# Delta rule of a two-block network: the chunk inverse as two 64-token diagonal blocks

## What is computed

```python
def _gdn_scan(q, k, v, log_a, beta, s0):
    g = jnp.cumsum(log_a.reshape(b, h, n, CHUNK), axis=-1)
    rel = g[..., :, None] - g[..., None, :]
    a = jnp.einsum('bhnid,bhnjd->bhnij', kc, kc) * bc * jnp.where(strict, jnp.exp(jnp.where(strict, rel, 0.0)), 0.0)
    rhs = jnp.concatenate([bc * vc, bc * jnp.exp(g)[..., None] * kc], axis=-1)
    sol = lax.linalg.triangular_solve(a + jnp.eye(CHUNK, dtype=a.dtype), rhs,
                                      left_side=True, lower=True, unit_diagonal=True)
    u, wk = sol[..., :dv], sol[..., dv:]
    ...
    def step(s, inp):
        v_new = u_n - jnp.einsum('bhck,bhkv->bhcv', w_n, s)
        s_next = jnp.exp(gl_n)[..., None, None] * s + jnp.einsum('bhck,bhcv->bhkv', kt_n, v_new)
        return s_next, (None if q is None else (v_new, s))
```

## Time and profile before

| | us |
|---|---|
| median of 3 runs (lowest, highest) | 3285.2 (3284.71, 3288.44) |
| profiled execution, first to last instruction | 3281.3 |
| PE busy | 2868.6 (87%) |
| DVE busy | 977.1 (30%) |
| POOL busy | 599.6 (18%) |
| ACT busy | 460.3 (14%) |
| the delta rule's stretch, 377.6 to 764.5 | 386.9 |

### The profile page before, as it was taken

The page is one execution under the profiler, slowest core; times in us unless marked ns, Lnnn a source line. Parts: engine busy times, 40 slices in busy tenths (PEclk is TensorE's granted clock), DMA queues, the critical chain, the costliest instruction groups (busy, mean ns, idle before and its releaser), DMA issues.

```text
span 3281.3 us, 34289 instructions
## 1 busy us (share of the span) xinstructions
PE 2868.6 (87%) x14021; PEld 1432.4 (44%) x14021; DVE 977.1 (30%) x1607; ACT 460.3 (14%) x959; POOL 599.6 (18%) x431
## 2 busy tenths in 40 slices
PE   5998699998998989997999789677888889889887
PEld 2644577774443555443454333344232233223232
DVE  2043555552113341111111258663111121121122
ACT  2012122221101211111111211341000000000000
POOL 0001255551200123433443210311000000000000
PEclk7999899999998899998999889888899999999999
DMA  5020243322312359997999721124899999999997
GB/s 228 26 77 0 68 132 125 123 94 109 115 51 99 138 213 384 374 383 263 388 375 364 279 83 51 36 99 164 323 421 421 421 421 421 421 421 421 421 421 292
DMA packets 127316, 793.24 MB, mean 242 GB/s; under 512 B 21795, under 2 KB 22179, under 8 KB 56761
## 3 DMA queue, kind: packets, MB, share of 16 engines
q1 hardware_dynamic: 102328, 744.31, 56.5%
q0 software_dynamic: 23008, 37.81, 4.8%
q10 hardware_dynamic: 1824, 8.91, 0.7%
HBM read 769.37 MB, written 38.86 MB: 246 GB/s over the span
## 4 chain that ended last, share of the span: by engine, by line
PE 58%; DMA 26%; DVE 8%; issue 3%; ACT 3%; POOL 1%; SPq 0%; POOLq 0%; ACTq 0%; DVEq 0%
DMA arena<-in_w_down 12%; PE b L2928 9%; DMA yd<-arena 8%; PE b L1389 5%; PE b L1825 4%; PE b L489 4%; DMA arena<-h2d,arena 3%; PE b L2963 3%; PE b L491 3%; PE b L2416 2%; PE b L630 2%; PE b L1839 2%; PE b L1077 2%; PE b L1090 2%; PE b L1453 2%
## 5 line engine op out<-in xcount | busy, mean ns | idle before, releaser
L2928 PE MATMUL b<-arena 128*64 128x512 f32 x2048 | 456.8, 603 | 17.9 <-DMA arena<-in_w_up 7.1
L1825 PE MATMUL b<-arena 128*64 128x256 f32 x3072 | 355.6, 384 | 2.9 <-DMA arena<-in_w_gu 1.6
L2943 PE MATMUL b<-arena 128*64 128x512 f32 x1024 | 244.7, 602 | 57.6 <-DMA arena<-in_w_down 57.3
L2928 PEld LDWEIGHTS b<-arena 128*64 128x64 f32 x2048 | 155.1, 138 | 315.7 <-issue 273.8
L1825 PEld LDWEIGHTS b<-arena 128*64 128x64 f32 x3072 | 213.0, 137 | 114.4 <-issue 4.6
L2142 POOL DMA_INDIRECT yd<-arena x96 | 152.5, 1588 | 344.0 <-ACT arena L1923 138.0
L1839 PE MATMUL b<-arena 128*64 128x512 f32 x768 | 186.0, 604 | 0.7 <-issue 0.7
L2098 DVE TENSOR_TENSOR arena<-arena,b 128x128 f32<-128x128 f32 x96 | 27.9, 290 | 515.1 <-ACT arena L1916 515.1
L1389 PE MATMUL b<-arena 128*128 128x512 f32 x384 | 167.0, 596 | 9.7 <-DMA arena<-in_w_in 9.7
L2943 PEld LDWEIGHTS b<-arena 128*64 128x64 f32 x1024 | 64.8, 135 | 236.8 <-DMA arena<-in_w_down 138.0
L3035 DVE TENSOR_TENSOR arena<-arena,b 128x512 f32<-128x512 f32 x32 | 20.6, 686 | 462.8 <-PE b L2928 462.8
(11 more groups left out here) (473 smaller groups left out, 3724.0 us busy)
## 6 DMA issues: line engine op xcount, KB each, us to landing
arena<-in_w_gu SPq DMA_DIRECT2D x65, 2048.0 KB, 13.1
arena<-in_w_gate SPq DMA_DIRECT2D x128, 1024.0 KB, 27.0
arena<-in_w_up SPq DMA_DIRECT2D x128, 1024.0 KB, 26.1
arena<-in_w_down SPq DMA_DIRECT2D x128, 1024.0 KB, 24.5
arena<-in_w_dn SPq DMA_DIRECT2D x65, 1024.0 KB, 10.4
arena<-in_w_mod SPq DMA_DIRECT2D x80, 512.0 KB, 3.8
arena<-in_w_in SPq DMA_DIRECT2D x19, 2048.0 KB, 8.4
arena<-yd SPq DMA_DIRECT2D x12, 512.0 KB, 8.9
```

The source lines that it names most:

```text
L1825: x = e.matmul(ps[i % 2][64 * j:64 * j + 64, 0:256], XGT[i % 2][:, k % 4, (k // 4) * 64:(k // 4) * 64 + 64], GUB[place_of(w)][:, k, j * 25 ...
L2928: x = e.matmul(ps[b + c][64 * hf:64 * hf + 64, :], XS[q % 2][:, kb, (n % 2) * 64:(n % 2) * 64 + 64], w[:, u * 512:(u + 1) * 512], start=(k ...
L2943: x = e.matmul(ps[4][64 * hf:64 * hf + 64, :], H[:, c * 4 + j, hi * 64:hi * 64 + 64], w[:, i * 1024 + hf * 512:i * 1024 + hf * 512 + 512], ...
```

## The change

The inverse is made of 64-token blocks. The two diagonal 64x64 blocks of each head's matrix go through the ladder's levels 1 to 5, each on its own half of the partitions, with X and XT side by side in one tile `XX` (4 heads x 64 columns each), so that one DVE subtraction takes both. Then level 6 makes the off-diagonal block alone, as two groups of four 64x64 products, which ACT writes with a minus sign into a full-size transposed inverse `XTF`. W is gone: keys times state (`KS`, phase 14, on PE) is scaled by -beta*exp(g) and added to the scaled values by DVE before the inverse is applied, and V is one product a head. Each tick now does the ladder's groups of all units first (`..._small`) and then the rest (`..._large`). LAG is 6, and there are 84 ticks. The level masks are 64 columns wide, and there are six levels of them, so the constants have 896 columns fewer. The decay differences are made with whole-tile DVE instructions in place of eight quarter ones, Q is moved to phase 3, and DVE clears the two `XTF` tiles once at the start.

The core of the diff:

```diff
-    for n, s in enumerate((1, 2, 4, 8, 16, 32, 64)):
-        same = (r // (2 * s)) == (c // (2 * s))
+    for n, s in enumerate((1, 2, 4, 8, 16, 32)):
+        same = (r64 // (2 * s)) == (c64 // (2 * s))
...
-    LAG, PHASES = 7, 18
+    LAG, PHASES = 6, 18
...
             for n, ph in under_way(tick):
-                pe_phase(e, n, ph)
+                for u in small_uses(n, ph):
+                    pe_small(e, n, u)
+            for n, ph in under_way(tick):
+                for u in large_uses(n, ph):
+                    pe_large(e, n, u)
             if tick < len(rows.pieces):
                 rows.pe(e, tick)
...
+        if kind == "P" and lv < 6:
+            e.wait_ge(*pool_.at(n, "BT", lv))
+            e.wait_ge(*dve.at(n, ("XX", lv - 1)))
+            for h in range(4):
+                for b in range(2):
+                    x = e.matmul(p[half(b), half(h)], BT[half(b), half(h)], X[half(b), half(h)], start=True, stop=True, skip_group_check=True)
+        elif kind == "P":
+            e.wait_ge(*dve.at(n, ("XX", 5)))
+            for h in range(4):
+                x = e.matmul(p[far, half(h)], B["off"][near, half(h)], X[near, half(h)], start=True, stop=True, skip_group_check=True)
+        elif lv < 6:
+            e.wait_ge(*act_.at(n, ("P", lv)))
+            for h in range(4):
+                for b in range(2):
+                    if lv < 5 or b == d:
+                        e.matmul(p[half(b), half(h)], XT[half(b), half(h)], P[half(b), half(h)], start=True, stop=True, skip_group_check=True)
+            for h in range(4):
+                for b in range(2):
+                    x = e.matmul(p[half(b), 256 + 64 * h:320 + 64 * h], P[half(b), half(h)], XT[half(b), half(h)], start=True, stop=True, skip_group_check=True)
...
-                x = e.matmul(p[:, hs(h)], B["bk"][:, hs(h)], B["XT"][:, hs(h)], start=True, stop=True)
...
+        elif u == "KS":
+            p = free(e, n, "KS")
+            e.wait_ge(*dve.at(n - 2, "S"))
+            for h in range(4):
+                x = e.matmul(p[:, hs(h)], KT[:, h, tsl], S_[d][:, hs(h)], start=True, stop=True)
...
             for h in range(4):
-                x = e.matmul(p[:, hs(h)], B["XT"][:, hs(h)], B["bv"][:, hs(h)], start=True, stop=(s == 0))
-                if s:
-                    x = e.matmul(p[:, hs(h)], B["wT"][:, hs(h)], S_[d][:, hs(h)], start=False, stop=True)
...
+                x = e.matmul(p[:, hs(h)], XTF[d][:, hs(h)], B["bv"][:, hs(h)], start=True, stop=True)
...
+            for b in range(2):
+                e.activation(h64(B["AA"][half(b), 256:512]), p[half(b), :, half(b)], ACT.Copy).then_inc(*act_.up(n, "blocksT", b))
+            e.activation(h64(B["off"][half(d), :]), p[half(d), :, half(1 - d)], ACT.Copy).then_inc(*act_.up(n, "T"))
...
+            e.tensor_tensor(heads(B["ET"]), heads(p[:, :]), per_row(B["g"], 4, 128), ALU.subtract).then_inc(*dve.up(n, "rel"))
+            e.wait_ge(*dve.now())
+            e.tensor_scalar(B["A"], B["ET"], 0.0, None, ALU.max).then_inc(*dve.up(n, "A"))
+            e.tensor_scalar(B["ET"], B["ET"], 0.0, None, ALU.min).then_inc(*dve.up(n, "ET"))
...
+            e.tensor_tensor(h64(B["BT"]), h64(B["AA"][:, 256:512]), by4(C[f"{mT}{lv}"]), ALU.mult).then_inc(*pool_.up(n, "BT", lv))
```

More of the change, by code:

```diff
@@ L995, in uses @@
             return ["g", "G"]
[L996 to L1010 removed]
+        if ph in (1, 2):
+            return ["KT"[ph - 1]]
+        if ph == 3:
+            return ["Q"] if t < 4 else []
+        if ph == 14:
+            return ["KS"] if s else []
+        if ph == 16:
+            return ["V"]
+        if ph == 17:
+            return (["O"] if t < 4 else []) + (["S"] if s < 5 else [])
+        return []
+    order = [(n, u) for tick in range(ticks) for uses in (small_uses, large_uses) for n, ph in under_way(tick) for u in uses(n, ph)]
     bank = {x: ps[i % 7] for i, x in enumerate(order)}
@@ L1018, in evacuated @@
             e.wait_ge(*act_.at(n, "EG"))
-        elif u in ("T", "W") or u[0] == "P" or (u == "O" and first[units[n][2]] == n):
+        elif u == "T" or u[0] == "P" or u == ("XX", 6) or (u == "O" and first[units[n][2]] == n):
             e.wait_ge(*act_.at(n, u))
@@ L1114, in pe_phase @@
         else:
             e.wait_ge(*dve.at(n, "V"))
[L1116 to L1126 removed]
+            p = free(e, n, "S")
@@ L1128, in act @@
+            for h in range(4):
+                x = e.matmul(p[:, hs(h)], B["kt"][:, hs(h)], B["vn"][:, hs(h)], start=True, stop=True)
+        x.then_inc(*mm.up(n, u))
     def act(e):
@@ L1131, in act, with act_small, act_large @@
             for n, ph in under_way(tick):
-                act_phase(e, n, ph)
-    def act_phase(e, n, ph):
+                for kind, lv in small_uses(n, ph):
+                    act_small(e, n, kind, lv)
+            for n, ph in under_way(tick):
+                act_large(e, n, ph)
+    def act_small(e, n, kind, lv):
+        s, d, t = units[n]
+        B = sets[n % 3]
+        p = bank[n, (kind, lv)]
+        if kind == "P":
+            r = slice(0, 128) if lv < 6 else half(1 - d)
+            e.wait_ge(*mm.at(n, ("P", lv)))
+            e.activation(B["A"][r, 0:256], p[r, 0:256], ACT.Copy).then_inc(*act_.up(n, ("P", lv)))
+        elif lv == 6:
+            r = half(d)
+            e.wait_ge(*mm.at(n, ("XX", 6)))
+            e.activation(heads(XTF[d])[r, :, half(1 - d)], h64(p[r, 0:256]), ACT.Copy, scale=-1.0).then_inc(*act_.up(n, ("XX", 6)))
+    def act_large(e, n, ph):
         s, d, t = units[n]
@@ L1162, in dve_, with dve_small, dve_large @@
         all_of(e, *K.ret)
+        for d in range(2):
+            e.memset(XTF[d], 0.0).then_inc(*dve.up("clear", d))
         for tick in range(ticks):
             for n, ph in under_way(tick):
-                dve_phase(e, n, ph)
+                dve_small(e, n, ph)
+            for n, ph in under_way(tick):
+                dve_large(e, n, ph)
             if tick < len(rows.pieces):
                 rows.take(e, tick)
-    def dve_phase(e, n, ph):
+    def dve_small(e, n, ph):
+        s, d, t = units[n]
+        B = sets[n % 3]
+        XX = B["XX"]
+        if ph == 3:
+            a = CCOLS["lev0" if d == 0 else "levT0"][0]
+            pair = K.CT[:, a:a + 128].rearrange("p (u o n) -> p u o n", u=2, o=1).broadcast_to([128, 2, 4, 64])
+            e.wait_ge(*act_.at(n, "blocksT", 1))
+            e.tensor_tensor(XX.rearrange("p (u h n) -> p u h n", u=2, h=4), B["AA"].rearrange("p (u h n) -> p u h n", u=2, h=4), pair,
+                            ALU.mult).then_inc(*dve.up(n, "X0"))
+            e.wait_ge(*dve.now())
+            e.tensor_tensor(XX.rearrange("p (a n) -> p a n", a=8), per_col(C["eye"], 8), XX.rearrange("p (a n) -> p a n", a=8),
+                            ALU.subtract).then_inc(*dve.up(n, ("XX", 0)))
+        elif 4 <= ph < 12 and ph % 2:
+            u = ("XX", (ph - 3) // 2)
+            e.wait_ge(*mm.at(n, u))
+            e.tensor_tensor(XX, XX, bank[n, u][:, :], ALU.subtract).then_inc(*dve.up(n, u))
+        elif ph == 13:
+            u = ("XX", 5)
+            p = bank[n, u]
+            e.wait_ge(*mm.at(n, u))
+            r = half(d)
+            e.tensor_tensor(XX[r, 0:256], XX[r, 0:256], p[r, 0:256], ALU.subtract).then_inc(*dve.up(n, "X5"))
+            if n >= 2:
+                e.wait_ge(*mm.at(n - 2, "V"))
+            else:
+                e.wait_ge(*dve.at("clear", d))
+            e.tensor_tensor(heads(XTF[d])[half(0), :, half(0)], h64(XX[half(0), 256:512]), h64(p[half(0), 256:512]), ALU.subtract).then_inc(*dve.up(n, "XT5"))
+            e.tensor_tensor(heads(XTF[d])[half(1), :, half(1)], h64(XX[half(1), 256:512]), h64(p[half(1), 256:512]), ALU.subtract).then_inc(*dve.up(n, u))
+    def dve_large(e, n, ph):
         s, d, t = units[n]
@@ L1173, in dve_phase @@
         endc = 127 if d == 0 else 0
-        mT = "levT" if d == 0 else "lev"
         if ph == 0:
```

222 lines of the change are left out of this document (91 added, 131 removed).

## The result

The changed kernel takes 3193.81 us (median of 4 runs, 3192.7 to 3198.59) where the kernel before takes 3284.95 (median of 4, 3267.33 to 3288.44). The ratio is 0.9732, with a 95% interval of 0.9712 to 0.9751, so it is 2.5 to 2.9% faster. The forecast was 3191, range 3170 to 3268. Executions that took far longer than the others of the same kernel (two of five in experiment 3, 5019.64 and 14586.62 us) are left out of all medians and ratios.

The account below looks back on a forecast made before the run. PE was taken to bound the delta rule, busy 371.7 of 386.9 us. Counts of 89 and 97 us gained gave 94, so 3281.3 to 3187 profiled, 3191 as median; own range 3172 to 3208, with rivals 3170 to 3268.

Parts of the forecast that it names:

- The ladder: Inverse's products on PE: two quarters side by side, 0.058 us a pair, 15.2 to 7.9 us a unit, 88 us gained.
- rival of single file: Ladder on PE: the two quarters do not run at once, ladder 14.4 us a unit, time 3267; chance 0.16.
- slower rival: Ladder on PE: 64-column loads not overlapped or quarter changes costly, 0.112 us a pass, about 3430 us; chance 0.06.
- Steady unit 23.2: PE's work for one unit in the steady stretch of the delta rule: 23.2 us, where 32.0 was measured before.
- change of form: PE switching array form between small, large and piece: about 0.10 us each, one more a tick, 8.4 us lost.
- Idle time: PE's waits in the stage: 8 us for unit starts, 4 at the start, 5 in the tail; 17 against 15, cost 2.
- second count: Delta rule stage added up stretch by stretch: 290 us against 386.9, 97 less, 98 with the start.
- rival of the clock: PE falls to 1.2 GHz for a third of the stage, costing about 50 us, time 3240; chance 0.04.
- The ring of pieces: Two buffers for pieces' transfers: 2.5 us a tick at best, hidden by mean tick 3.9; about 1 us in second unit.
- The start of the youngest unit: Chain from G to the older unit's BT: 5.3 us, even with PE's work, no margin; 8 us of stalls allowed.
- The start of the program: Smaller constants arrive earlier, so the stage starts 0.7 us earlier, between 0 and 1.1.
- First count: Sum of gains and losses: 88 + 10.7 - 8.4 - 2 + 0.7 = 89 us.

Follow-up runs that it names:

- experiment 3: Changed kernel with its units 7 ticks apart instead of 6, timed: 3209.69 us, ratio 0.9793 to the kernel before.
- experiment 9: Changed kernel with ACT's first exponential waiting for the clamping of A alone: 3192.12 us, ratio 0.9736 to the kernel before.
- experiment 4: Changed kernel with 12 more 64x64 products a unit on the idle quarter of the array, results unread: 3186.62 us, ratio 0.9725 to the kernel before.
- experiment 2: Kernel before with keys times state (`KS`) in place of W, old ladder and distance kept: 3278.25 us, ratio 0.9989 to the kernel before.
- experiment 7: Changed kernel with a third buffer for the modulation pieces: 3190.86 us, ratio 0.9728 to the kernel before.
- experiments 8: Changed kernel with the decay differences made again by eight quarter DVE instructions: 3202.84 us, stage 6.8 us longer.
- experiment 11: Changed kernel with a third buffer for pieces and ACT's exponential of A waiting for its own clamping alone: 3186.5 us, ratio 0.9725 to the kernel before.
- experiment 6: Changed kernel with each group's eight passes of one quarter first, then the other's eight: 3220.03 us, stage 26.7 us longer.

## Why the prediction was right

**PE as the bound.** Right. A steady unit is 23.20 us, all of it busy, and in experiment 9 a shorter chain leaves it as long.

**The ladder, 0.058 us a pair of passes.** Right, by the pace of the XX groups and by experiment 4. The rows of 64-column loads and of pairs on halves of the array, carried over to quarters. The Trainium skill, "TensorEngine Tiling (Array Packing)", section "Gotcha 1: PSUM Pressure", says that different row tiles cannot access one bank at the same time, from which I had worked out the single file. The measurement is against it for this pattern, in which the two quarters write different partitions: 0.058 us a pair, and 24 more passes on the idle quarter for 0.0 us. The rival of single file (3267) falls with it, and the slower rival too.

**Steady unit 23.2.** Measured 23.2, in part by errors that cancel. W and `KS` gave 0.9 of a unit's 32.0 in experiment 2, though 8.1 instead of 10.7 us in the stage. A change of form costs more than the 0.10 that I took: two P groups take 1.07 us for 0.93, and K between small products and a piece 1.09 for 0.895, so two changes there are 0.2. Against it stands an overlap that my count of passes group by group had left out: P 6, which works on one quarter, and the P of the next unit take 0.90 us together, where as many passes in file, with a change of form, take 1.07 (rows in the last section).

**Idle time, 17 us forecast.** Mis-sized, 20.0 measured, and made otherwise than I had put it. The stretches of the second count against the trace, with tick ends taken from the pieces:

| ticks | forecast | measured |
|---|---|---|
| first six | 19 | 19.1 |
| next five sixes | 102 | 103.6 |
| six steady units | 141.6 | 141.5 |
| six of the two last units | 17 | 18.0 |
| last six, one unit | 11 | 15.8 |
| sum | 290.6 | 298.0 |

Two thirds of the miss are the last six ticks. My chain there had the copies, products and handovers, but neither the last two pieces, for one of which PE waits 1.3 us, nor the clock: O takes some 3.4 us, twice what it takes in a steady unit. The 141.5 for six steady units is luck in part: the 0.4 us of stall a unit that I had put there for the youngest unit's chain did not come, and two waits for finished modulation rows (1.0 and 1.4 us) took their place. The rival of the clock was thus true in small, in the tail alone and for under 2 us, not the 50 that it was given.

**The ring of pieces.** The term that failed by the largest factor: "costs about 1 us" in the second unit. Measured are 8.4 us of waits in eight places. The first, 2.5 us, is for the very first piece and was there before (2.3), so 5.8 are new: 3.4 in the first unit, 0.3 in the second, 2.2 in the last twelve ticks. I had held the ring's 2.5 us a tick against the mean tick of 3.9 and against the second unit alone. But a transfer is issued only when the piece two before its own is done, and has the tick before its own and most of its own to land. In the first and last ticks of the trace a transfer takes 3.6 to 4.9 us from its issue, which comes 0.6 to 1.1 us after the last pass of that piece starts; the waits stand where two neighbouring ticks are shorter than both together. Experiment 7 gets 2.6 us back in the stage. Two waits are left there, one of 2.4 us for the first piece, which either ring asks for only when the stage begins, and one of 1.8.

**The start of the youngest unit.** "Even, with no margin" was right to 0.2 us (experiments 8 and 9), though its parts are not: as I listed them they already make 5.1 us, which leaves 0.2 of the 5.3 for all handovers, and the clampings are 0.43 and 0.42 where I took 0.6 each, as the nearest full tiles on DVE with two tensors to read (0.69). The Trainium skill, "VectorE: DVE Perf Modes", section "Mode 2×_2P — use both read ports for one tensor", gives operations with one tensor in SBUF twice the pace in float32; 0.43 beside 0.69 goes that way, though not all of it. The 8 us that I allowed for it were too many, since PE's wait for level 0 (L1221) is 1.8 us in the whole stage, and no wait for BT is named in its list. (One wait of P, 0.9 us at 403.40, has no releaser named; it is 0.94 in experiment 7 and 0.60 with the shorter chain of experiment 11, so it belongs to this chain.) The pieces and 4.9 us of waits for DVE's taking of finished modulation rows (L645), for which I had no term, made up the rest.

**The start of the program.** 0.4 us earlier (377.3 for 377.7), forecast 0.7 between 0 and 1.1. That says little: over the traces read here the stage starts at 376.7 to 378.2 with the constants of before and at 374.7 to 379.8 with the new ones. The constants land after 28.2 us where it was 29.3, and the chain of waits now leads to x, which lands after 33.4 where it was 34.3. DMA issue rows, then the chain of waits at the program's start:

```profile
arena<-in_consts SPq DMA_DIRECT2D x1, 1564.5 KB, 28.2
```

```profile
4.28 33.35 DMA arena<-in_x
```

**The stretch behind.** Keeps its length, 2508.0 and 2508.1 us, with the wait for its first weights 9.1 where it was 9.7.

**The sum.** First count 89, second 97, taken 94, measured 89.6 in the profiled execution. The first count came out closer, with errors that cancel in it. PE's busy time in the stage fell by 93.7 us (371.7 to 278.0), where the ladder, W and the changes of form make 90.3; its idle time rose by 4.8, where I had 2. The medians lie 91.1 us apart (3284.95 and 3193.81), and the forecast of 3191 is 3 us below the measured one.

## What to carry to other kernels

Triangular blocks of 64 paid on TensorE here because products of the two diagonal quarters follow each other closely, in turns of two to four passes; the same products in runs of eight lost 27 of the 89 us. Before units are packed closer, what has a fixed time is to be held against the shortest stretch that it has, not the mean: here the ring's transfer against two neighbouring ticks, and the chain of the last unit alone. And an instruction that is off the bound by 0.2 us looks the same in the busy times as one that is off by 2; only the chain from one release to the next shows it.

## What was unexpected of the hardware

**TensorE starts passes out of the program's order, over a short distance.** In experiment 6 a pass of L1089 starts at 579.67 and one of L1086, ahead of it in the program, at 579.73. The changed kernel's own trace has it too, where P 6 of one unit (L1080, eight passes on one quarter) stands ahead of P of the next (L1076):

```profile
554.78 0.50 PE L1080 MATMUL b<-arena 64*64 64x64 f32 x5
555.07 0.27 PE L1076 MATMUL b<-arena 64*64 64x64 f32 x2
555.12 0.22 PE L1080 MATMUL b<-arena 64*64 64x64 f32 x1
...
555.68 1.16 PE L1128 MATMUL b<-arena 128*128 128x128 f32 x8
```

P starts with the fifth pass of P 6, ahead of three of them, and the two groups are through after 0.90 us. By the kernel's slices the quarter of P 6 shares its rows with one of P's two quarters and its columns with the other, and they write different banks. How far TensorE reaches is not shown to be a fixed number of passes: in experiment 4, where P 6 has sixteen passes on two quarters, P starts ahead of six. With runs of 2, 4 and 8 passes a quarter, two P groups with their change of form take 1.07, 1.13 and 1.47 us. The Trainium skill, "TensorE: Matmul & The Clock Gate", section "The mechanism", has matrix products start and end strictly in program order, with weight loads alone pulled ahead. The starts in these traces don't agree with it; ends are modelled in these records, so of them nothing is shown.

**Two quarters write one bank at once**, at 0.058 us for a pair of passes, the pace of one alone. The pairs tried share neither rows nor columns and write different partitions of the bank: the two diagonal quarters, and in experiment 4's P 6 and XX 6 the other two. Quarters that write the same partitions of one bank at the same time were not tried.
